# The opening of a hybrid decoder step on one core: first two strips by halves, mean square in the third strip

## What is computed

```
def _rmsnorm(x, g):
    y = x * rsqrt(mean(x * x, axis=-1) + NORM_EPS)
    return y * g
...
h = _rmsnorm(x, gn[0]);  z = h @ w_in;  q = _rope(z[..., q columns], pos)
```

## Time and profile before

| | |
|---|---|
| median of 3 runs | 1013.47 us |
| the profiled execution | 1013.51 us |
| its span, first to last instruction | 1011.7 us |
| PE busy | 987.4 us (98%) |
| DVE busy | 593.6 us (59%) |
| ACT busy | 435.6 us (43%) |
| mean granted clock of PE over the span | 0.994 |

### The profile page before, as it was taken

The page is one execution under the profiler, slowest core; times in us unless marked ns, Lnnn a source line. Parts: engine busy times, 40 slices in busy tenths (PEclk is TensorE's granted clock), DMA queues, the critical chain, the costliest instruction groups (busy, mean ns, idle before and its releaser), DMA issues. The chain is left out here.

```text
span 1011.7 us, 17609 instructions
## 1 busy us (share of the span) xinstructions
PE 987.4 (98%) x7496; PEld 902.5 (89%) x7496; DVE 593.6 (59%) x744; ACT 435.6 (43%) x552; POOL 35.4 (3%) x68
## 2 busy tenths in 40 slices
PE   7999999989999999999999999999999999999996
PEld 7988999655999999999997878789799999999996
DVE  6756643547477554334685776586673685553343
ACT  5222233566556554333443452526344655543331
POOL 0310000000000000000001000000100000000000
PEclk9999999999999999999999999999999999999998
DMA  9987859636525444444554958675664254444421
GB/s 354 353 291 252 280 163 357 233 125 209 219 86 206 166 166 166 167 166 166 202 200 156 336 188 323 238 266 195 263 258 165 109 182 166 167 166 166 166 83 47
DMA packets 50701, 206.62 MB, mean 204 GB/s; under 512 B 3536, under 2 KB 3920, under 8 KB 35024
## 3 DMA queue, kind: packets, MB, share of 16 engines
q1 hardware_dynamic: 45216, 182.58, 51.1%
q0 software_dynamic: 5424, 23.15, 6.1%
HBM read 181.39 MB, written 24.33 MB: 203 GB/s over the span
## 5 line engine op out<-in xcount | busy, mean ns | idle before, releaser
L587 PE MATMUL banks<-hH,wH 128*128 128x288 f32 x1248 | 376.1, 301 | 4.6 <-DVE hL L1596 3.7
L1218 ACT ACTIVATE wH<-raw 128x2048 fp32r<-128x2048 f32 x116 | 222.3, 1916 | 361.6 <-PE banks L589 359.0
L1587 DVE TENSOR_TENSOR wL<-raw,wH 128x2048 fp32r<-128x2048 f32 x113 | 258.8, 2291 | 188.5 <-ACT wH L1218 188.2
L589 PE MATMUL banks<-hH,wL 128*128 128x288 f32 x1248 | 368.8, 295 | 0.0
L588 PE MATMUL banks<-hL,wH 128*128 128x288 f32 x1248 | 368.5, 295 | 0.0
L587 PEld LDWEIGHTS banks<-hH,wH 128*128 128x128 f32 x1248 | 236.5, 189 | 23.1 <-issue 12.8
L588 PEld LDWEIGHTS banks<-hL,wH 128*128 128x128 f32 x1248 | 235.6, 189 | 0.4
L589 PEld LDWEIGHTS banks<-hH,wL 128*128 128x128 f32 x1248 | 235.2, 188 | 0.0
L589 PE MATMUL banks<-aH,wL 128*128 128x288 f32 x512 | 151.8, 296 | 0.0
L587 PE MATMUL banks<-aH,wH 128*128 128x288 f32 x512 | 151.3, 296 | 0.0
L588 PE MATMUL banks<-aL,wH 128*128 128x288 f32 x512 | 149.3, 292 | 0.0
(11 more groups left out here) (273 smaller groups left out, 1038.3 us busy)
## 6 DMA issues: line engine op xcount, KB each, us to landing
raw<-wst SPq DMA_DIRECT2D x120, 1024.0 KB, 4.9
cache_sb<-kcache SPq DMA_DIRECT2D x14, 1024.0 KB, 6.2
sslot<-state SPq DMA_DIRECT2D x11, 1024.0 KB, 7.3
sstate_out<-sslot POOLq DMA_DIRECT2D x11, 1024.0 KB, 6.6
raw<-vcache SPq DMA_DIRECT2D x6, 1024.0 KB, 9.5
w_area<-vcache SPq DMA_DIRECT2D x6, 1024.0 KB, 13.0
raw<-state SPq DMA_DIRECT2D x5, 1024.0 KB, 7.5
sstate_out<-raw POOLq DMA_DIRECT2D x5, 1024.0 KB, 5.5
```

Source lines behind the costliest of these rows:

```text
L587: nc.tensor.matmul(out[:, m, :], wH[:, u % 2, c], hi[:, k, :], start=first, stop=False)
L589: return nc.tensor.matmul(out[:, m, :], wL[:, u % 2, c], hi[:, k, :], start=False, stop=last)
L1218: nc.scalar.activation(wH[:, at % SPL, :], raw[:, raw_slot(at), :], ACT.Copy).then_inc(h_round, 1)
L1587: nc.vector.tensor_tensor(wL[:, at % SPL, :], raw[:, raw_slot(at), :], wH[:, at % SPL, :].bitcast(F32), ALU.subtract).then_inc(l_split, 1)
```

## The change

It has five parts. SP loads the first half of `x` in two parts and strip 1 in two halves. The warming products go from 14 to 20. Strips 0 and 1 are multiplied by halves of `k`, the products that need only high parts first, with waits of their own on each half. ACT and DVE handle strip 1 in halves. ACT's squares and DVE's sums move behind their work on strip 2, and the mean square moves on PE from strip 1 into strip 2, behind its first column half.

```diff
-N_RUN_FIRST = 14
+N_RUN_FIRST = 20
...
+            first, second = slice(0, HALF_STRIP), slice(HALF_STRIP, KT * SC)
+            sp.dma_start(raw[:, 0, first], wst[MIX_ORDER[0]][:, first]).then_inc(half_landed, 16)
+            sp.dma_start(x[:, 0:2, :], x_in[:, 0:2, :]).then_inc(x_landed, 16)
+            sp.dma_start(x[:, 2:4, :], x_in[:, 2:4, :]).then_inc(x_landed2, 16)
+            sp.dma_start(raw[:, 0, second], wst[MIX_ORDER[0]][:, second]).then_inc(w_landed[0], 16)
+            sp.dma_start(x[:, 4:8, :], x_in[:, 4:8, :]).then_inc(x_landed3, 16)
+            sp.dma_start(raw[:, 1, first], wst[MIX_ORDER[1]][:, first]).then_inc(half_landed2, 16)
+            sp.dma_start(raw[:, 1, second], wst[MIX_ORDER[1]][:, second]).then_inc(w_landed[1], 16)
...
+                for half in range(2):
+                    ks = range(4 * half, 4 * half + 4)
+                    pe.wait_ge(h_round if half else half_round, 1)
+                    for k in ks:
+                        pe.wait_ge(hx_round, k + 1)
+                        for m in range(2):
+                            part_product(0, out, wH, hH, m, k, start=k == 0)
+                    pe.wait_ge(l_split if half else half_split, 1)
+                    for k in ks:
+                        for m in range(2):
+                            part_product(0, out, wL, hH, m, k)
+                    for k in ks:
+                        pe.wait_ge(hx_split, k + 1)
+                        for m in range(2):
+                            mm = part_product(0, out, wH, hL, m, k, stop=k == KT - 1)
...
             def second_product(out):

-                pe.wait_ge(l_split, 2)
+                for half in range(2):
+                    ks = range(4 * half, 4 * half + 4)
+                    pe.wait_ge(h_round if half else w1_round, 1 + half)
                     for m in range(2):
+                        for k in ks:
+                            part_product(1, out, wH, hH, m, k, start=k == 0)
+                            part_product(1, out, wH, hL, m, k)
+                    pe.wait_ge(l_split if half else w1_split, 1 + half)
+                    for m in range(2):
+                        for k in ks:
+                            mm = part_product(1, out, wL, hH, m, k, stop=k == KT - 1)
+                mm.then_inc(strip_used, 1)
...
+            def third_product(out):
+
+                pe.wait_ge(l_split, 3)
                 for m in range(2):
                     for k in range(KT):
-                        mm = tile_product(1, out, hH, hL, m, k)
-                        if (m, k) == (0, 6):
-                            pe.wait_ge(mats_in, 16)
-                            mean_square(mean_d, sumsq[:, :], x0_sum, 3)
+                        mm = tile_product(2, out, hH, hL, m, k)
+                    if m == 0:
+                        pe.wait_ge(mats_in, 16)
+                        mean_square(mean_d, sumsq[:, :], x0_sum, 3)
...
-            round_strip(1, 1)
+            act.wait_ge(half_landed2, 16)
+            nc.scalar.activation(wH[:, 1, first], raw[:, 1, first], ACT.Copy).then_inc(w1_round, 1)
+            act.wait_ge(w_landed[1], 16)
+            nc.scalar.activation(wH[:, 1, second], raw[:, 1, second], ACT.Copy).then_inc(h_round, 1)
+            round_strip(SPL, SPL)
             for c in (slice(0, KT // 2), slice(KT // 2, KT)):
                 nc.scalar.activation(y[:, c, :], x[:, c, :], ACT.Square).then_inc(xsq0, 1)
-            round_strip(SPL, SPL)
             root(0)
```

More of the change, by code:

```diff
@@ L355, in build_program @@
         half_landed, x_landed2, x0_sum, xsq0 = map(sem, ("half_landed", "x_landed2", "x0_sum", "xsq0"))
+        half_landed2, x_landed3, w1_round, w1_split = map(sem, ("half_landed2", "x_landed3", "w1_round", "w1_split"))
         mix_round, mix_split = sem("mix_round"), sem("mix_split")
@@ L605, in first_product @@
                     nc.tensor.matmul(banks[0:64, 6, 0:N_COL], col[:, 0:64], col[:, 0:N_COL], start=True, stop=True)
[L606 to L610, removed]
-                    for m in range(2):
-                        mm = tile_product(0, out, hH, hL, m, k)
+                for half in range(2):
[13 more added lines that the diff above has]
+                            mm = part_product(0, out, wH, hL, m, k, stop=k == KT - 1)
@@ new lines, in first_product, with part_product, second_product @@
+                mm.then_inc(strip_used, 1)
+            def part_product(u, out, w, h, m, k, start=False, stop=False):
+                c = slice(k * SC + m * P, k * SC + m * P + P)
+                return nc.tensor.matmul(out[:, m, :], w[:, u % 2, c], h[:, k, :], start=start, stop=stop)
+            def second_product(out):
+                for half in range(2):
+                    ks = range(4 * half, 4 * half + 4)
+                    pe.wait_ge(h_round if half else w1_round, 1 + half)
+                    for m in range(2):
+                        for k in ks:
[5 more added lines that the diff above has]
+                            mm = part_product(1, out, wL, hH, m, k, stop=k == KT - 1)
@@ L613, in first_product @@
                 mm.then_inc(strip_used, 1)
-            def second_product(out):
-                pe.wait_ge(l_split, 2)
+            def third_product(out):
+                pe.wait_ge(l_split, 3)
                 for m in range(2):
                     for k in range(KT):
-                        mm = tile_product(1, out, hH, hL, m, k)
-                        if (m, k) == (0, 6):
-                            pe.wait_ge(mats_in, 16)
-                            mean_square(mean_d, sumsq[:, :], x0_sum, 3)
+                        mm = tile_product(2, out, hH, hL, m, k)
+                    if m == 0:
+                        pe.wait_ge(mats_in, 16)
+                        mean_square(mean_d, sumsq[:, :], x0_sum, 3)
@@ L700, in in_mix @@
                     second_product(G(j))
+                elif p == 2:
+                    third_product(mix_bank(j))
                 else:
@@ L1310, in _ @@
             act.wait_ge(relu_sq, 1)
-            for arrived, done, c, arrived2, first in ((half_landed, half_round, slice(0, HALF_STRIP), x_landed, 0),
-                                                      (w_landed[0], h_round, slice(HALF_STRIP, KT * SC), x_landed2, KT // 2)):
+            first, second = slice(0, HALF_STRIP), slice(HALF_STRIP, KT * SC)
+            act.wait_ge(half_landed, 16)
+            nc.scalar.activation(wH[:, 0, first], raw[:, 0, first], ACT.Copy).then_inc(half_round, 1)
+            for arrived, k in ((x_landed, 0), (x_landed2, 2)):
                 act.wait_ge(arrived, 16)
[L1314 to L1317, removed]
-            round_strip(1, 1)
+                round_x(k, 0, 0)
+                round_x(k + 1, 0, 0)
+            act.wait_ge(w_landed[0], 16)
+            nc.scalar.activation(wH[:, 0, second], raw[:, 0, second], ACT.Copy).then_inc(h_round, 1)
+            act.wait_ge(x_landed3, 16)
+            for k in range(KT // 2, KT):
+                round_x(k, 0, 0)
+            act.wait_ge(half_landed2, 16)
[3 more added lines that the diff above has]
+            round_strip(SPL, SPL)
             for c in (slice(0, KT // 2), slice(KT // 2, KT)):
                 nc.scalar.activation(y[:, c, :], x[:, c, :], ACT.Square).then_inc(xsq0, 1)
-            round_strip(SPL, SPL)
             root(0)
@@ L1730, in _ @@
                     split_x(0, k, 0, 0)
-            split_strip(1, 1)
+            for ready, count, c, done in ((w1_round, 1, slice(0, HALF_STRIP), w1_split),
+                                          (h_round, 2, slice(HALF_STRIP, KT * SC), l_split)):
+                dve.wait_ge(ready, count)
+                nc.vector.tensor_tensor(wL[:, 1, c], raw[:, 1, c], wH[:, 1, c].bitcast(F32), ALU.subtract).then_inc(done, 1)
+            split_strip(SPL, SPL)
             dve.wait_ge(xsq0, 2)
@@ L1737, in _ @@
                 nc.vector.tensor_tensor(out, y[:, 0:n, :], y[:, n:2 * n, :], ALU.add).then_inc(x0_sum, 1)
-            split_strip(SPL, SPL)
             pre_norm(0)
```

## The result

The changed kernel takes 1018.23 us (median of 6 runs, 1017.42 to 1019.11) against 1013.48 (6 runs, 1013.01 to 1014.16): 1.0046 times as long, 95% interval 1.0034 to 1.0059, or 4.75 us slower. The forecast was 1017.4. The profiled execution of the changed kernel took 1018.96 us (span 1017.2, against 1011.7), so its rows show some 0.7 us more than the median does. The six executions fall into two threes: 1018.58 to 1019.11 us with a mean granted clock of 0.992, and 1017.42 to 1017.88 with 0.995. The median lies between them, and the profiled execution is one of the longer.

What follows compares the result with a forecast made beforehand. PE, busy 98% of the span, was taken as the bound, with its waits and slow-clock stretches. Strip 3 2.4 us later plus 1.5 us of slow clock made 3.9 on 1013.5: 1017.4 us, range 1016.5 to 1019.2.

Steps and rivals of the forecast that it cites:

- The mechanism: Faster strips 0 to 2, then a late mean square delays strip 3's low part; PE idles 5.1 us, then runs slow.
- Part 1, warming: Opening: six more warming products, 1.0 to 1.7 us, end warming at 7.8 to 8.5 us, taken as 7.8; path unchanged.
- Parts 2 to 4: Strips 0 to 2: strip 1 starts at 14.7 us instead of 17.31, strip 2 at 21.05 instead of 24.21.
- The fixed cost of added loads: SP's load queue: each added load costs 1.9 us, strip 2 starts at 24.8, end some 1021 us; a rival, chance 4%.
- fixed 2.0 us: Skill page's fixed time per DMA; by it two added loads would put off strip 1's end by an estimated 4 us.
- 1.74 us of the prediction: Time by which 576 KB landed after the first half strip; taken to show queued loads overlap and land by bytes.
- The clock term: Strip 3 after the idle wait: some 14 products at 1.2 GHz, each 0.11 us dearer, 1.5 us.
- rival (a): The clock stays at 2.4 GHz over the wait; POOL's copies set the cached scores: +3.4, 1016.9 us; chance 14%.
- The sum: Whole kernel: strip 3 starting 2.4 us later plus 1.5 us of slow clock, 3.9 us slower, 1017.4 us.
- rival (b): Opening: added warming doesn't work, clock falls near 9.3 us as before, everything behind strip 0 1.3 us later: 1018.7 us; chance 9%.
- Rival (d): Strip 3's low part isn't late, done by 27.9 us where strip 2 ends; the kernel takes 1010.9 us; chance 3%.

Runs made afterwards that it cites:

- first experiment: The kernel before with only the squares, sums and mean square moved behind strip 2's work and into strip 2: 1021.91 us against 1013.36, 1.0080 times.
- fourth experiment: The changed kernel with squares and sums ahead of strip 2's work and the mean square back in strip 1: 1012.53 us against 1013.36, 0.9991 times.
- fifth experiment: The changed kernel with strip 3's rounding ahead of the root and its low part ahead of the reciprocal: 1016.86 us against 1013.39, 1.0035 times.
- filled wait: The changed kernel with 30 more products keeping PE busy while it waits for strip 3's low part: 1016.94 us against 1013.36, 1.0035 times.
- second experiment: The kernel before with 20 warming products instead of 14 and nothing else: 1013.43 us against 1013.36, 0.9999 times.

## Why the prediction was right

**The mechanism held at each step.** The slow opening went, the mean square came after 24 products of strip 2, the wait for strip 3's low part was 4.9 us (forecast 5.1), and products 0.24 apart followed. The first experiment shows that the late mean square is enough for it, the fourth that the loss goes when it alone is put back, the fifth that the same lateness also holds POOL's copies.

**Part 1, warming, was mis-sized, and cost little.** I ended it at 7.8 us, with 8.5 as the far bound; it ended at 2.73 + 6.30 = 9.03, so strip 0 started at 8.96. The passes kept the pace that the earlier trace rows show early in the run. The pace differs between executions: 40 passes took 6.30 us here and 5.21 in the kernel with warming alone. All later steps came some 0.7 us behind my figures: strip 2 at 21.75 (forecast 21.05), mean square 24.91 (24.2), low part 33.46 (32.83), strip 3 33.61 (32.95). Most of that is not the warming. The first half strip could be rounded only from 6.45, where the earlier trace rows have 5.99. With 14 products strip 1 starts 15.04 - 6.31 = 8.73 us behind the start of that rounding, close to the 14.7 - 5.99 = 8.71 of the forecast; here it is 15.40 - 6.45 = 8.95. So the late warming added some 0.2 us and the later first half strip some 0.5. When that half strip is there differs between executions, from 5.51 (fifth experiment) to 6.45, and it was 6.33 with the old loads of the first experiment.

**Parts 2 to 4 held otherwise.** Strip 0 had no holes, since the late start left ACT ahead of PE: 6.44 us for 48 products. Strip 1 ran without a wait. The fixed cost of added loads did not show: the second half of `x` was rounded from 10.69, when it was there, against 10.42 before, while the first half strip itself came 0.46 later, and the mean square waited for its turn, not for the sums (done at 23.8). Strip 2's load was there at 17.00 instead of 16.5, as late as the first half strip was. The fixed 2.0 us that the prediction takes from the Trainium skill's page "DMA: Bandwidth & Descriptors" stand there in the section "Anatomy of one DMA — SWDGE (gpsimd) path", which is about loads that GpSimd issues. The loads here are issued by SP, so the 1.74 us of the prediction decide this case, but do not refute the page.

**The clock term was too small.** I took 1.5 us for strip 3, and with POOL's copies ending at nearly the same time only 0.5 of it reached the sum: 3.9 against the 3.4 of rival (a). In the profiled execution strip 3 took 42.59 - 33.61 = 8.98 us, against 6.39 before (36.91 - 30.52): 2.6 us. At the median, the filled wait leaves 4.75 - 3.58 = 1.2 us to the clock. That this is also what parts the two threes of the changed kernel's executions is likely, but not shown: one of the six was kept as a trace.

**The sum:** in the profiled execution 3.1 us later at strip 3, and 2.6 more from its slow products, 5.7 against the 3.9 of the forecast. At the median 4.75, of which the wait and the copies make 3.6 (forecast 3.4) and the clock 1.2 (forecast 0.5). The path was right, and the clock's price on it was put at under half. That the median, 0.8 us above the forecast, still lies in the range is in part luck: the upper end was set for rival (b), which did not come about. Rival (a), a clock that stays up, is what the filled wait shows: 3.6 us slower against my 3.4. Rival (d) fell on the point that was to decide it: the low part was not there by strip 2's end, by 4.9 us. What stays open is rival (b) on its own terms: with 14 products in the changed kernel the opening was no slower, so no run here shows that the changed kernel needs the six.

## What to carry to other kernels

When a step of a serial chain is moved later on one engine, go through every queue that it feeds and find what stands behind its result; here the mean square, with the squares and sums that feed it, was moved by one strip, and DVE's next low part and POOL's copies both stood behind it. What a start-up wins is worth only as much as the next thing that is late lets through: measure each part alone and with the one that holds it (warming alone gave nothing, and 1.7 us at strip 3 became 0.8 until the copies were out of the way). An idle stretch of PE can cost twice, once as a wait and once more in the products behind it: the 4.9 us here did, the 1.56 us of the second experiment did not.

## What the runs showed of the hardware that was not expected

- After an idle 4.9 us, products ran at 1.2 GHz (granted clock 0.50) for some 5.4 us (33.61 until about 39.0), longer than the 3 us and more of the opening before the change.
- How long warming takes is not fixed by its count: 40 passes took 6.30 us in one execution and 5.21 in another, 28 took 4.02 and 4.80.
- POOL's first eight copies took 4.91 to 4.93 us in every run, where they stood beside DVE's ropes and splits (from 31.12 in the fourth experiment, 35.87 after, rows 10 before). The next eight in the kernel before took 2.78, most of it while DVE was idle (POOL's row, then DVE's on either side of it):

```profile
42.12 2.78 POOL L540 COPY vtok<-qT 32x64 f32<-32x64 f32 x8 [5.63 <-DVE qT L1678]
...
41.60 0.45 DVE L1678 TENSOR_TENSOR qT<-sqacc 128x288 f32<-128x288 f32 x1
...
44.51 0.76 DVE L1671 TENSOR_TENSOR sqacc<-banks,trigs 128x576 f32<-128x576 f32 x1 [2.46 <-PE banks L589]
```

The Trainium skill's page "GPSIMD Engine Reference", section "Specifications", says that the engine shares its interfaces to the local memory with VectorE, with contention when VectorE takes two inputs from there. The rows agree with it, but do not show that it is the cause: the splits (`wL<-raw,wH`) and the second half of each rope (`qT<-sqacc`) take two, the first half of each rope takes one of its two from `banks`, where PE's results stand.

The copies mattered here: in the fourth experiment PE stood idle for 0.73 us until they were done.
